# The first adaLN job in two quarters: loads, order of the opening, and two matmul groups moved

## What is computed

```python
mod_ctx = silu_cctx @ w_ada[i] + b_ada[i]          # 1024 -> 3 * 1024
mod_lat = silu_c @ w_ada[i] + b_ada[i]
...
shift, scale, gate = jnp.split(mod, 3, axis=-1)
h = rms_norm(x, norm_w) * (1 + scale[:, None]) + shift[:, None]
proj = h @ w_in
```

## Time and profile before

| what | value |
|---|---|
| median of 3 runs | 1401.28 us |
| the profiled execution's own time | 1401.26 us |
| its span in the profile | 1399.5 us |
| PE busy | 1387.0 us, 99% of the span |
| POOL and DVE busy | 1029.1 us (74%) and 1027.1 us (73%) |
| ACT busy | 467.1 us (33%) |
| granted TensorE clock, mean | 0.999 |

### The profile page before, as it was taken

The page is one execution under the profiler, slowest core; times in us unless marked ns, Lnnn a source line. Parts: engine busy times, 40 slices in busy tenths (PEclk is TensorE's granted clock), DMA queues, the critical chain, the costliest instruction groups (busy, mean ns, idle before and its releaser), DMA issues.

```text
span 1399.5 us, 27040 instructions
## 1 busy us (share of the span) xinstructions
PE 1387.0 (99%) x10101; PEld 1331.1 (95%) x10101; DVE 1027.1 (73%) x1503; ACT 467.1 (33%) x1039; POOL 1029.1 (74%) x1421
## 2 busy tenths in 40 slices
PE   8999999999999999999999999999999999999997
PEld 5899999999999999999998999999999999999997
DVE  6988679665677688999978766976566776869234
ACT  5432123214766333001252323241266661320122
POOL 3789886696554499998869898657765546979763
PEclk9999999999999999999999999999999999999999
DMA  9362665123766555444334455722346665453222
GB/s 366 126 151 76 191 167 159 61 66 127 188 179 192 177 204 212 150 151 155 106 136 122 107 165 149 192 86 61 106 135 191 193 173 201 139 190 120 76 76 91
DMA packets 198047, 206.85 MB, mean 148 GB/s; under 512 B 76592, under 2 KB 163760, under 8 KB 196784
## 3 DMA queue, kind: packets, MB, share of 16 engines
q1 hardware_dynamic: 116000, 155.13, 35.6%
q10 hardware_dynamic: 81936, 50.16, 12.4%
HBM read 179.23 MB, written 26.02 MB: 147 GB/s over the span
## 4 chain that ended last, share of the span: by engine, by line
PE 98%; DVE 1%; DMA 0%; SPq 0%; issue 0%; ACT 0%; DVEq 0%; ACTq 0%
PE acc L718 79%; PE X L684 5%; PE acc L684 3%; PE X L972 2%; PE X L952 2%; PE X L988 1%; PE X L1013 1%; PE acc L866 1%; PE X L981 1%; DVE p_lo L1606 1%; DMA ada_pre<-in_wada 0%; DVE ssq L1581 0%; PE X L825 0%; DVE xr L2143 0%; PE X L910 0%; PE acc L732 0%
## 5 line engine op out<-in xcount | busy, mean ns | idle before, releaser
L617 POOL CAST w_hi<-w_st 128x256 fp32r<-128x256 f32 x696 | 410.5, 604 | 337.1 <-PE acc L718 162.2
L621 POOL TENSOR_TENSOR w_lo<-w_st,w_hi 128x256 fp32r<-128x256 f32 x696 | 645.0, 936 | 0.0
L718 PE MATMUL acc<-h_hi,w_hi 128*128 128x320 f32 x1696 | 402.1, 318 | 0.0
L718 PE MATMUL acc<-h_lo,w_hi 128*128 128x320 f32 x1696 | 386.3, 309 | 0.0
L718 PE MATMUL acc<-h_hi,w_lo 128*128 128x320 f32 x1696 | 386.2, 309 | 0.0
L718 PEld LDWEIGHTS acc<-h_hi,w_hi 128*128 128x128 f32 x1696 | 284.4, 188 | 14.7 <-issue 11.8
L718 PEld LDWEIGHTS acc<-h_hi,w_lo 128*128 128x128 f32 x1696 | 283.5, 188 | 0.0
L718 PEld LDWEIGHTS acc<-h_lo,w_hi 128*128 128x128 f32 x1696 | 283.4, 188 | 0.0
L1824 DVE SCALAR_TENSOR_TENSOR cv<-raw,convw_sb,cv 128x642 f32<-128x642 f32 x128 | 137.2, 1072 | 4.5
L1540 DVE SCALAR_TENSOR_TENSOR ada_acc<-ada_st,sc,ada_acc 128x512 f32<-128x512 f32 x112 | 107.8, 1002 | 1.8
L1280 ACT ACTIVATE cvt<-cv 128x642 f32<-128x642 f32 x32 | 23.8, 744 | 158.1 <-DVE cv L1824 158.1
(11 more groups left out here) (264 smaller groups left out, 2322.5 us busy)
## 6 DMA issues: line engine op xcount, KB each, us to landing
w_st<-in_wts SPq DMA_DIRECT2D x174, 512.0 KB, 3.7
cum_bc<-cum_dram ACTq DMA_DIRECT2D x80, 256.0 KB, 5.0
ada_st<-in_wada SPq DMA_DIRECT2D x34, 512.0 KB, 4.3
ex_bc<-ex_dram ACTq DMA_DIRECT2D x64, 128.0 KB, 3.1
ada_pre<-in_wada SPq DMA_DIRECT2D x14, 512.0 KB, 8.9
xs<-xs_dram SPq DMA_DIRECT2D x64, 80.0 KB, 3.8
mga_dram<-c_buf SPq DMA_DIRECT2D x16, 320.0 KB, 5.2
xf<-xf_dram SPq DMA_DIRECT2D x4, 1280.0 KB, 7.1
```

The source lines that it names most:

```text
L617: nc.gpsimd.tensor_copy(quarter(w_hi, slot, q), quarter(w_st, slot, q)).then_inc(s_pool, 1)
L621: nc.gpsimd.tensor_tensor(quarter(w_lo, slot, q), quarter(w_st, slot, q), f(quarter(w_hi, slot, q)), ALU.subtract).then_inc(w_split, 1)
L718: last = mm(a[:, hf, 0:n1], w[:, s, cols], x[:, k, hf * HALF:hf * HALF + n1], start=(k == 0 and n == 0), stop=(k == KC - 1 and n == 2))
```

## The change

Job 0 becomes two jobs of 256 columns each. `JOBS_FIRST` now has five entries and `JOB_COLS` says which channel chunks each one gives: job 0 gives amul of k = 0..1, job 1 of k = 2..3, job 2 (the former job 1) of k = 4..7, jobs 3 and 4 are the shift. The first quarter is loaded alone at the head of the queue (`lead_ada(0)`, four loads of 256 KB whose rows have 1 KB), the second after x 0-1 and the first halves of both weight tiles. `first_mm(0)` waits for all four of its loads, where before it began with half of them. On PE, `first_mm(1)` and `first_tp(1)` of the second quarter stand right behind chunks (0,0) and (0,1), one filler goes from behind `dt_part(0,0)` to behind (1,1), one filler ahead of `first_mm(0)` and the one inside it go away and one behind `first_tp(0)`; `dt_part(0,1)` comes ahead of (1,4), and (1,4), (1,5) ahead of `stat_mm(0)`; (0,6) comes ahead of `stat_bc(0)`. On ACT the row copies of the jobs come ahead of squares. On DVE the first part of dt comes ahead of `add_square(0, 4)`, and `add_square(0, 5)` behind dt's second part. alog is loaded later, with a semaphore of its own. The other edits only count the fifth job.

```diff
-JOBS_FIRST = [(0, q, h) for q in (1, 0) for h in (0, 1)]
+JOBS_FIRST = [(0, 1, 0), (0, 1, 0), (0, 1, 1), (0, 0, 0), (0, 0, 1)]
+JOB_COLS = (slice(0, 2), slice(2, 4), slice(4, 8), slice(0, 4), slice(4, 8))
...
+    ada_lead = place("ada_lead", [P, 4, 2, 512], r_h)
...
+        def lead_ada(quarter):
+
+            L, q, hf = JOBS_FIRST[quarter]
+            for n in range(4):
+                sp.dma_start(ada_lead[:, n, :, lead_cols(quarter)], wada[L, q, hf, n, :, :, lead_cols(quarter)])\
+                    .then_inc(pre_in[quarter], 16)
...
-        first_ada(0)
+        lead_ada(0)
         sp.dma_start(bada_sb[:, :, :], bada).then_inc(norm_in, 16)
         sp.dma_start(normw_sb[:, :, :], normw).then_inc(norm_in, 16)
-        sp.dma_start(ea[:, :], alog).then_inc(norm_in, 16)
+        first_x(0)
         half_weight(0, 0)
-        first_x(0)
+        half_weight(1, 0)
+        lead_ada(1)
         first_x(1)
-        half_weight(1, 0)
-        first_ada(1)
+        first_ada(2)
         first_x(2)
         dt_weight(0)
         half_weight(0, 1)
         half_weight(1, 1)
         first_x(3)
-        first_ada(2)
+        sp.dma_start(ea[:, :], alog).then_inc(ea_in, 16)
+        first_ada(3)
         sp.wait_ge(w_split, FIRST_SPLIT[0][-1])
         weight(2, 0)
-        first_ada(3)
-        sp.wait_ge(row_mm, 2)
+        first_ada(4)
+        sp.wait_ge(row_mm, 3)
...
-            chunks((1, 0), (1, 1), (0, 2))
             first_mm(1)
-            chunks((1, 2))
+            chunks((1, 0))
             first_tp(1)
-            chunks((0, 3), (1, 3))
+            chunks((1, 1))
+            keep_pace(1, X[0])
+            chunks((0, 2), (1, 2))
+            first_mm(2)
+            chunks((0, 3))
+            first_tp(2)
+            chunks((1, 3))
             dt_part(0, 0)
-            keep_pace(1, X[0])
-            chunks((0, 4), (0, 5), (1, 4))
+            chunks((0, 4), (0, 5))
             pe.wait_ge(x_in, 16)
             dt_part(0, 1)
+            chunks((1, 4), (1, 5))
             stat_mm(0)
-            first_mm(2, range(DTG))
+            first_mm(3, range(DTG))
+            chunks((0, 6))
             stat_bc(0)
-            chunks((0, 6))
             chunks((0, 7)).then_inc(tile_done, 1)
-            first_mm(2, range(DTG, KC))
-            chunks((1, 5))
-            first_tp(2)
+            first_mm(3, range(DTG, KC))
             chunks((1, 6))
+            first_tp(3)
             chunks((1, 7)).then_inc(tile_done, 1)
...
-        keep_pace(4)
-        first_mm(0, range(DTG))
-        keep_pace(1)
-        first_mm(0, range(DTG, KC))
+        keep_pace(3)
+        first_mm(0)
         keep_pace(2)
         first_tp(0)
-        keep_pace(4)
+        keep_pace(3)
...
         row_copy(0)
-        for k in range(KC // 2):
-            if k % 2 == 0:
-                act.wait_ge(x_part[k // 2], 16)
-            first_p(k)
-        for k in range(KC // 2):
-            square(0, k, xr[:, k, :])
+        act.wait_ge(x_part[0], 16)
+        first_p(0)
+        first_p(1)
+        row_copy(1)
+        square(0, 0, xr[:, 0, :])
+        square(0, 1, xr[:, 1, :])
+        act.wait_ge(x_part[1], 16)
+        first_p(2)
+        first_p(3)
+        square(0, 2, xr[:, 2, :])
+        square(0, 3, xr[:, 3, :])
+        row_copy(2)
         act.wait_ge(x_part[2], 16)
         square(0, 4, xr[:, 4, :])
-        row_copy(1)
         square(0, 5, xr[:, 5, :])
...
         job_out(0)
-        for k in range(KC // 2):
-            first_low(k)
-        for k in range(KC // 2):
-            add_square(0, k)
+        first_low(0)
+        first_low(1)
+        job_out(1)
+        add_square(0, 0)
+        first_low(2)
+        first_low(3)
+        add_square(0, 1)
+        add_square(0, 2)
+        add_square(0, 3)
...
+        dt_scaled(0, 0, DTG)
+        job_out(2)
         add_square(0, 4)
-        dt_scaled(0, 0, DTG)
-        job_out(1)
-        add_square(0, 5)
         first_low(4)
         first_low(5)
         dt_scaled(0, DTG, KC)
+        add_square(0, 5)
         add_square(0, 6)
         add_square(0, 7)
         first_low(6)
```

More of the change, by code:

```diff
@@ L346, in build @@
     consts_in, consts_made, x_in = sem("consts_in"), sem("consts_made"), sem("x_in")
-    norm_in, x_part = sem("norm_in"), [sem(f"x_part{i}") for i in range(KC // 2 - 1)]
+    ea_in, norm_in, x_part = sem("ea_in"), sem("norm_in"), [sem(f"x_part{i}") for i in range(KC // 2 - 1)]
     again_in = sem("again_in")
@@ L352, in build @@
     ada_used, ada_mm = sem("ada_used"), sem("ada_mm")
-    pre_in = [sem(f"pre_in{i}") for i in range(2 * NF)]
+    pre_in = [sem(f"pre_in{i}") for i in range(2 * (NF - 1))]
     row_mm, row_out, job_read = sem("row_mm"), sem("row_out"), sem("job_read")
@@ L390, in build, with lead_cols, job_width @@
     s_act, s_dve, s_pool = sem("s_act"), sem("s_dve"), sem("s_pool")
+    def lead_cols(quarter):
+        return slice(256 * quarter, 256 * (quarter + 1))
     def ada_first(n):
         return ada_pre[n][:, :, :] if n < len(ada_pre) else ada_st[:, n - len(ada_pre), :, :]
+    def job_width(n):
+        return JOB_COLS[n].stop - JOB_COLS[n].start
     def job_rows(n):
-        return acc[0][:, 0, :] if n == 0 else X[2][:, :]
+        return (acc[0][:, 0, :] if n == 0 else X[2][:, :])[:, 0:P * job_width(n)]
     DT_FIRST = (X[3][:, 0:HALF], X[1][:, 0:HALF], X[1][:, HALF:HALF + 2])
@@ L513, in first_ada @@
             L, q, hf = JOBS_FIRST[job]
-            for n in range(4 * job, 4 * job + 4):
+            for n in range(4 * (job - 1), 4 * job):
                 sp.dma_start(ada_first(n), wada[L, q, hf, n % 4, :, :, :]).then_inc(pre_in[n // 2], 16)
+        def lead_ada(quarter):
[3 more added lines that the diff above has]
+                    .then_inc(pre_in[quarter], 16)
         def first_x(i):
@@ L760, in shifts @@
             def shifts(half):
-                pe.wait_ge(job_read, 3 + half)
+                pe.wait_ge(job_read, NF - 1 + half)
                 for t in range(RAWT):
@@ L797, in opening @@
             tile(2, p_hi, p_lo, ready=ready,
[L798 removed]
+                 hooks=[(2, lambda: first_mm(4)), (4, lambda: first_tp(4)), (6, first_shifts), (8, last_shifts)])
         def job_mm(n):
@@ L817, in first_mm @@
             pe.wait_ge(sc_ready, 1)
-            at = 4 * n
+            at = 4 * (n - 1)
             if n >= 1:
                 pe.wait_ge(job_read, n)
+            if n < 2:
+                pe.wait_ge(pre_in[n], 64)
             for k in ks:
                 j = k % DTG
[L823 to L826, removed]
+                if n < 2:
+                    rows = ada_lead[:, k // 2, k % 2, lead_cols(n)]
+                else:
+                    rows = ada_first(at + k // 2)[:, k % 2, :]
+                    if j == 0:
+                        pe.wait_ge(pre_in[(at + k // 2) // 2], 32)
+                last = mm(job_rows(n)[32 * j:32 * j + 32, :], scp[:, k, :], rows, start=(k < DTG), stop=(k >= DTG))
             if k == KC - 1:
@@ L834, in first_tp @@
                 pe.wait_ge(job_read, n)
-            for j in range(4):
+            for j in range(job_width(n)):
                 for b in range(4):
@@ L1564, in job_out @@
             dve.wait_ge(ada_mm, n + 1)
-            cols = slice(4 * hf, 4 * hf + 4)
-            total = X[2][:, 0:8].rearrange("p (v j) -> p v j", v=2)
+            cols = JOB_COLS[n] if n < NF else slice(4 * hf, 4 * hf + 4)
+            k0, k1 = cols.start, cols.stop
+            total = X[2][:, 0:8].rearrange("p (v j) -> p v j", v=2)[:, :, 0:k1 - k0]
             TT(mods[:, 3 * L + q, :, cols], total,
-               bada_sb[:, 3 * L + q, cols].unsqueeze(1).broadcast_to([P, 2, 4]), ALU.add).then_inc(job_read, 1)
+               bada_sb[:, 3 * L + q, cols].unsqueeze(1).broadcast_to([P, 2, k1 - k0]), ALU.add).then_inc(job_read, 1)
             dve.wait_ge(job_read, n + 1)
             if q == 1 and (n < NF or hf == 1):
-                k0, k1 = (4 * hf, 4 * hf + 4) if n < NF else (0, KC)
+                if n >= NF:
+                    k0, k1 = 0, KC
                 STT(out=amul[:, L, :, k0:k1], in0=mods[:, 3 * L + 1, :, k0:k1], scalar=1.0,
```

26 lines of the change are left out of this document (13 added, 13 removed).

## The result

The changed kernel takes **1404.95 us** (median of 11 runs, 1404.49 to 1405.75), the kernel before 1401.28 (11 runs, 1400.85 to 1402.86): ratio 1.0026, 95% interval 1.0017 to 1.0034. It is slower by 3.7 us, and slower by more than the 0.2% that a measurement can tell. The forecast was 1402.8 us, the range ended at 1404.0.

A forecast was written before the change was run, and what follows sets the result against it. PE, busy 99% of the span, was taken to bound the kernel. A ledger of PE's lead or lag (-2.8, +0.6, +1.3, +0.5, +1.0, +0.8) gave about +1.5 on 1401.26: 1402.8 us, range 1400.6 to 1404.0.

The forecast's parts named there:

- start, first chunk: At the opening, the first quarter lands at 6.6 us and the first chunk starts at 11.0 instead of 13.80: -2.8 us.
- p_lo of k = 0 and 1: On DVE for the first chunks, p_lo runs beside POOL, two taking 3.1 us instead of 2.2: +0.6 us for PE.
- the quarter in the stream: Half of job 0's products, now behind two chunks on PE, with small matmuls and switches of matmul kind: +1.3 us.
- waits for the second quarter: After chunk (1,1), PE waits about 0.1 us for p_hi and 0.4 for p_lo: +0.5 us.
- waits at k = 4 and 5: PE waits 0.7, 0.6 and 0.2 us for p_lo and dt's second part, against 0.46 before: +1.0 us.
- stat_bc and hrows: stat_bc comes at 34.9 us, DVE's list starts 2.4 later and recovers 0.7, PE waits for hrows: +0.8 us.
- short rows cost little; I take 6.6: First quarter's load at the opening: 1 KB rows hardly slow it, so its last piece lands at 6.6 us.
- lie under transfers that fill the engines: SP's queue at the opening: four more load issues of 0.46 us each are hidden and cost nothing.
- rival 4: First load lands at 8 us or later because time goes with number of loads, not bytes: 1404.2 us; chance 0.07.
- by the row it stays: First products: TensorE taken at full speed despite the clock rule, keeping 1402.8 us instead of the rule's 1404.2.
- rival 3: TensorE slow at the first job, products about 2 us instead of 1: +1.4 on the forecast, 1404.2 us; chance 0.10.
- rival 1: DVE's list ahead of hrows recovers 1.5 us or more, so PE does not stop there: 1401.9 us; chance 0.20.

The follow-up runs named there:

- E3: Changed kernel with each quarter loaded by two transfers of 512 KB instead of four of 256 KB, same 1 KB rows; 1403.26 us, ratio 1.0016.
- E5: Changed kernel with two loads per quarter, four fillers first, tile 0's half ahead of x 0-1, tile 1's half behind the second quarter; 1402.98 us.
- E12: E5 with five fillers instead of four ahead of the first products; 1403.13 us, ratio 1.0014.
- E1: Changed kernel with five fillers instead of three ahead of the first products; 1404.84 us, ratio 1.0025.
- E4: Changed kernel with the last part of PE's stream ordered as in the kernel before, two interruptions fewer; 1404.93 us, ratio 1.0026.
- E6: Kernel before with only the last part of PE's stream ordered as in the change; 1401.98 us against 1401.26, ratio 1.0004.
- E8: Changed kernel with DVE's order of the kernel before at k = 4, ACT keeping the new order; 1405.58 us, ratio 1.0030.
- E9: Kernel before with only DVE's order changed: second job's rows ahead of dt's first part, square 5 behind dt's second; 1401.07 us, ratio 0.9998.
- E11: Kernel before with its first job loaded by eight transfers of 256 KB in 1 KB rows; 1404.77 us, ratio 1.0024.
- E7: Changed kernel with the small loads bada and normw moved behind x 0-1 and the first half of tile 0; 1405.57 us, ratio 1.0030.

## Why the prediction was wrong

The ledger, by its own steps; the measured column is PE's timeline of the changed kernel against the earlier trace rows:

| step | forecast | measured |
|---|---|---|
| start, first chunk | -2.8 | +0.26 |
| p_lo of k = 0 and 1 | +0.6 | +0.5 (0.87 against 0.08 + 0.30) |
| the quarter in the stream | +1.3 | +1.24 (17.36 to 18.37 and 19.45 to 19.68) |
| waits for the second quarter | +0.5 | +0.6 (0.17 + 0.19, and the filler 0.59 against 0.35) |
| waits at k = 4 and 5 | +1.0 | 0.0 (0.42 against 0.46) |
| more interruptions | not in the sum | +1.04 (19.39 against 18.35) |
| stat_bc and hrows | +0.8 | +0.14 (0.85 against 0.71) |
| sum | +1.4 to +1.5 | +3.78; tile 2, ahead of `hrows`, starts 3.65 later, and the spans differ by 3.8 |

*Start.* This is the step that failed, by 3.1 us: the first chunk came at 14.06 us instead of 11.0. Two terms make that up. The load landed at 7.57 us instead of 6.6, and from the landing to the first chunk it took 6.5 us instead of 4.4.

For the load, "short rows cost little; I take 6.6" came from one load alone in its window, and the number of loads was put at nothing, since they "lie under transfers that fill the engines". Those transfers did not fill them (198 GB/s from 5.3 to 6.3 us, against 414 in the kernel before), and with two loads the quarter landed at 6.63 to 6.67 (E3, E5, E12). That time goes with the number of loads was rival 4's mechanism, with a chance of 0.07; it named 8 us or later.

From landing to chunk, "by the row it stays" failed, for the speed of TensorE: the products took 1.93 us instead of 1.07 and four filler instructions 2.08 instead of 1.13, 1.8 us in all. That was rival 3, with a chance of 0.10. E1 shows that the engine alone did not set the start, since the weights came at the same time. Why the engine was slow stays open. The Trainium skill, "TensorE: Matmul & The Clock Gate" (Part 1: The HAM clock gate), whose rule the forecast weighed and left out of its sum, also says that what the first instructions cost varies from run to run; the runs agree (last section).

*The stream.* The quarter and its waits were right within 0.1 us each. Left out, without a reason, was that a series of chunks pays about 0.2 us each time other matmuls break into it: a chunk between other work takes 1.08 us from start to start (18.37 to 19.45), one inside a series 0.89. Up to tile 2 the kernel before has seven series, the changed one twelve. The forecast put 0.2 us for the quarter's two breaks into its 1.3 and none for the others; in the measured column all of them stand under interruptions. Five more at 0.2 make the 1.04. Two runs confirm the size: two breaks fewer gave 0.35 us (E4), two more cost 0.27 (E6 against the kernel before, added up in the same way). The first twelve instructions have no part in it: without the waits they took 2.4 to 2.5 us in both kernels.

*k = 4 and 5.* PE was itself some 3 us late there, so the rows were in time. In E3, E5 and E12, where PE is not late, 1.1 to 1.4 us of waits appear: the forecast's 1.5 in all for this place (0.7, 0.6 and 0.2) was sound in sum, and it was hidden behind the loss at the start.

*stat_bc and hrows.* The sign was right, the size not. In the kernel before with this part alone (E6) the list took back 1.0 us instead of 0.7, the breaks made PE later, and the stop cost 0.5 us instead of 0.8. In the changed kernel the list took 21.46 us instead of 22.77, and PE lost 0.14: rival 1's mechanism.

So the total is 2.1 us off while the start alone is off by 3.1: the start and the breaks cost more than forecast, k = 4 and 5 and `hrows` less. E3, whose first chunk at 11.37 us is nearest to the forecast's 11.0, took 1403.26 us, 0.5 more than forecast. That nearness is in part luck: 1.0 us of breaks that the sum lacks stand against most of the 0.8 for `hrows` that did not come.

**What the change is worth.** With the start mended (E12) the first chunk is 2.1 us earlier than before and the profile's span 1.5 longer (1401.0 against 1399.5). Behind the first chunk 1.24 us went to the quarter, about 1.0 to the breaks, 0.24 to the filler and 1.0 more to waits. The third job's last load lands at 21.01 us there, against 19.28 for the second job before, though as many bytes are ahead of it. But PE does not wait for it: the second half of the products, which needs it, starts at 21.55. The waits come behind, where p_lo of k = 4 follows these products, their rows and square 4 on DVE (24.72 to 26.05). How much of an earlier start a shorter way from products to p_lo would keep was not tried. No part of the change is shown to pay by itself: E8 sets DVE's order against ACT's, and E9 cannot be told from the kernel before.

## What to carry over

Halving a transfer halves its bytes, not its time: count what a transfer costs in the form it will have, with its rows and its number, and count the later loads on the same queue, which all move back. Before paying in the stream for an earlier start, follow the next job from its load to the first chunk that needs its rows: here 0.9 of the 2.1 us won at the start went into waits for those (E12). When a part is to be tried by itself, undo it on every engine that it touches (E8). And count the breaks in a series of matmuls as a price of their own, here 0.2 us each.

## What the runs showed of the hardware that was not expected

- A row of 1 KB took 46 ns on a DMA engine, one of 4 KB 159 (medians of the trace's records): 16% more for the same bytes. The Trainium skill, "DMA: Bandwidth & Descriptors" (Why small descriptors are slow), gives every packet a fixed cost on top of its bytes, and the trace agrees in sign. The larger price here, that of the number of transfers, is E3's and E11's.
- TensorE's speed at the first products is no constant of the code. With four fillers the first eight products of 512 columns took 1.07 us in the kernel before, 1.90 in E6 and 1.63 in E9, which have the same opening. The sixteen of 256 took 1.93 with three fillers in the changed kernel and 1.38 in E3, 1.93 with four in E5, and 1.07 with five in both runs. What decides stays open. The granted clock is shown at its upper level (2.4 GHz) all the while, as in this window of the changed kernel (columns as above), where the products and fillers ran at half the rate of later ones:

```profile
7.70:11.50 3.80, 3.79 (x20) 1.83 (x20) 0.00 (x0) 0.38 (x1) 0.31 (x1) 1.00 1.00 351
```

- The same four loads at the head of the queue landed at 7.31 to 7.92 us with two small loads behind them and at 9.11 in the one execution with x 0-1 directly behind (E7). That the load behind did this is not shown.
